# Index scores of a sparse-attention layer: two heads at once on 64 rows each, three products in place of two full-height ones

## What is computed

```python
dots = jnp.einsum('bqhd,bsd->bqhs', qi_b, k_idx) * idx_scale      # 8 index heads of 64
score = jnp.einsum('bqh,bqhs->bqs', wi_b, jax.nn.relu(dots))      # sum over the heads
score = jnp.where(causal, score, -jnp.inf)
_, sel = lax.top_k(score, topk)                                   # 256 keys per query
```

## Time and profile before

| | us |
|---|---|
| median of 3 runs | 732.51 (732.18 to 734.01) |
| the profiled execution | 737.07 |
| its span | 735.3 |
| TensorE matmul busy | 669.7 (91%) |
| TensorE weight loads busy | 552.7 (75%) |
| VectorE busy | 492.1 (67%) |
| ScalarE busy | 364.9 (50%) |
| GpSimd busy | 235.4 (32%) |

### The profile page before, as it was taken

One profiled execution on the slowest core, in us unless ns is written; L12 is line 12 of the kernel. 1 busy time (PEld: TensorE's weight loads), 2 busy tenths in 40 slices (PEclk: granted clock), 3 DMA queues, 4 the chain that ended last, 5 costly groups with the idle time before them and its releaser, 6 DMA issues.

```text
span 735.3 us, 8771 instructions
## 1 busy us (share of the span) xinstructions
PE 669.7 (91%) x3170; PEld 552.7 (75%) x3170; DVE 492.1 (67%) x737; ACT 364.9 (50%) x550; POOL 235.4 (32%) x113
## 2 busy tenths in 40 slices
PE   0489999899999999999999989998999988979996
PEld 0478988678888888888888877886777666758885
DVE  4786815677888899998079550014898988485734
ACT  1484435555563143452444434535787787783212
POOL 0003324432224152757766488420011110030000
PEclk9999999999999999999999999998999999989998
DMA  8902287353222110111100462075744340301531
GB/s 343 412 26 86 63 212 141 114 171 113 90 86 87 57 56 32 57 36 50 58 29 29 137 196 69 1 171 163 239 115 116 87 115 9 107 29 58 172 115 57
DMA packets 22661, 79.14 MB, mean 108 GB/s; under 512 B 3738, under 2 KB 4058, under 8 KB 21596
## 3 DMA queue, kind: packets, MB, share of 16 engines
q1 hardware_dynamic: 22620, 78.60, 35.2%
HBM read 61.77 MB, written 13.41 MB: 102 GB/s over the span
## 4 chain that ended last, share of the span: by engine, by line
PE 79%; DVE 8%; ACT 5%; issue 5%; DMA 2%; SPq 0%; ACTq 0%; DVEq 0%
PE ps L631 17%; PE ps L632 17%; PE ps L633 17%; PE ps L810 4%; PE ps L812 4%; PE ps L811 4%; PE ps L748 3%; DMA wa<-in_w_ada 2%; PE ps L689 2%; PE ps L690 2%; PE ps L670 2%; PE ps L671 2%; DVE phL L1384 2%; DVE acc L1178 1%; PE ps L761 1%
## 5 line engine op out<-in xcount | busy, mean ns | idle before, releaser
L631 PE MATMUL ps<-hH,wH 128*128 128x512 f32 (+1 forms) x592 | 230.3, 389 | 3.8 <-ACT wH L865 2.3
L632 PE MATMUL ps<-hL,wH 128*128 128x512 f32 (+1 forms) x592 | 228.3, 386 | 0.0
L633 PE MATMUL ps<-hH,wL 128*128 128x512 f32 (+1 forms) x592 | 228.1, 385 | 0.0
L1533 POOL TENSOR_TENSOR wL<-raw,wH 128x1024 fp32r<-128x1024 f32 x37 | 94.4, 2552 | 186.5 <-ACT wH L865 186.5
L631 PEld LDWEIGHTS ps<-hH,wH 128*128 128x128 f32 x592 | 111.9, 189 | 25.1 <-issue 3.0
L633 PEld LDWEIGHTS ps<-hH,wL 128*128 128x128 f32 x592 | 111.9, 189 | 21.5
L632 PEld LDWEIGHTS ps<-hL,wH 128*128 128x128 f32 x592 | 112.1, 189 | 19.2
L1376 DVE CUSTOM_DVE_ANT_0 ps<-ps,bias 128x128 f32<-128x128 f32 (+3 forms) x64 | 48.7, 761 | 45.6 <-PE ps L671 43.7
L1384 DVE TENSOR_TENSOR phL<-ps,phH 128x512 fp32r<-128x512 f32 (+1 forms) x96 | 52.7, 555 | 22.6 <-ACT phH L1040 18.5
L1020 ACT ACTIVATE relu<-ps,wabs 128x384 f32<-128x384 f32 (+5 forms) x48 | 40.1, 849 | 43.6 <-PE ps L690 17.5
L1270 DVE SCALAR_TENSOR_TENSOR score<-relu,wsgn,score 128x384 f32<-128x384 f32 (+5 forms) x42 | 49.7, 1183 | 17.2 <-ACT relu L1020 14.5
(11 more groups left out here) (206 smaller groups left out, 1102.9 us busy)
## 6 DMA issues: line engine op xcount, KB each, us to landing
raw<-in_w_units SPq DMA_DIRECT2D x36, 512.0 KB, 3.3
wa<-in_w_ada SPq DMA_DIRECT2D x8, 1024.0 KB, 8.8
ks<-qk_halves SPq DMA_DIRECT2D x32, 256.0 KB, 5.5
xin<-in_x SPq DMA_DIRECT2D x8, 512.0 KB, 12.5
gw<-in_w_ada SPq DMA_DIRECT2D x8, 512.0 KB, 4.4
qs<-qk_halves SPq DMA_DIRECT2D x16, 256.0 KB, 4.0
wo<-in_w_out SPq DMA_DIRECT2D x8, 512.0 KB, 9.3
xe<-in_x SPq DMA_DIRECT2D x8, 512.0 KB, 4.1
```

What stands on the lines that cost most here:

```text
L631: pe.matmul(out, wH[:, n % 2, kt, :], hH[:, kt, cols], start=(kt == 0), stop=False)
L632: pe.matmul(out, wH[:, n % 2, kt, :], hL[:, kt, cols], start=False, stop=False)
L633: mm = pe.matmul(out, wL[:, n % 2, kt, :], hH[:, kt, cols], start=False, stop=(kt == KT - 1))
L1533: g.tensor_tensor(wL[:, n % 2, :, :], raw[:, n % NRAW, :, :], wH[:, n % 2, :, :].bitcast(F32), ALU.subtract).then_inc(s_wL, 1)
```

## The change

The two heads of a pair are computed at once. `iqs` now has, for a pair of heads, the even head's rows in partitions 0 to 63 and the odd head's in 64 to 127, with the high and the low parts side by side in the free dimension and not over each other. `index_scores(i, pair)` makes three products per part of up to 512 keys: high by high, low by high and high by low; the fourth, low by low, is left out. Each is done for the even head on rows 0 to 63 into banks 4 and 5, then for the odd one on rows 64 to 127 into banks 6 and 7, in turn. The loop in `unit` issues a pair where it issued the even head, so pairs stand after steps 1, 5, 9 and 13 (block 2: 5, 8, 11 and 14). A pair waits for `s_relu` to reach u, so for both ReLUs of the pair before. The rotated rows come back by four DMAs.

```diff
-        iqs = at("iqs", [P, NIH, S - IQ0], F32R, 113)
+        iqs = at("iqs", [P, NIH // 2, 2, S - IQ0], F32R, 113)
...
-                                dst = iqs[HD * half + d:HD * half + d + k, h, :].bitcast(F32)
+                                dst = iqs[HD * (h % 2) + d:HD * (h % 2) + d + k, h // 2, half, :].bitcast(F32)
...
                     for half in range(2):
-                        sp.dma_start(iqs[HD * half:HD * half + ROPE, :, :].bitcast(F32),
-                                     diq[half].rearrange("h r s -> r h s")).then_inc(s_iqr, 16)
+                        for e in range(2):
+                            sp.dma_start(iqs[HD * e:HD * e + ROPE, :, half, :].bitcast(F32),
+                                         diq[half].rearrange("(p e) r s -> e r p s", e=2)[e]).then_inc(s_iqr, 16)
...
                         while b and at_step > first and scored * (2 * KT - first) < blocks * NIH * (at_step - first):
-                            index_scores(b + scored // NIH, scored % NIH)
-                            scored += 1
+                            index_scores(b + scored // NIH, scored % NIH // 2)
+                            scored += 2
...
-            def index_scores(i, h):
+            def index_scores(i, pair):
                 n = (i + 1) * P
-                u = NIH * (i - 2) + h
+                u = NIH * (i - 2) + 2 * pair
                 if u == 0:
                     pe.wait_ge(s_kidup, 16 * 8)
-                    pe.wait_ge(s_iqr, 32)
+                    pe.wait_ge(s_iqr, 64)
...
-                if u >= 2:
-                    pe.wait_ge(s_relu, u - 1)
-                dst = two(4 + 2 * (u % 2))
+                else:
+                    pe.wait_ge(s_relu, u)
                 for o in range(0, n, HALF):
                     e = min(n, o + HALF)
-                    q = iqs[:, h, P * i - IQ0:P * i - IQ0 + P]
-                    pe.matmul(dst[:, o:e], q, iks1[:, o:e], start=True, stop=False)
-                    mm = pe.matmul(dst[:, o:e], q, iks2[:, o:e], start=False, stop=True)
-                mm.then_inc(s_idx, 1)
+                    for m, (part, keys) in enumerate(((0, iks1), (1, iks1), (0, iks2))):
+                        for half in range(2):
+                            r = slice(HD * half, HD * half + HD)
+                            mm = pe.matmul(two(4 + 2 * half)[:, o:e], iqs[r, pair, part, P * i - IQ0:P * i - IQ0 + P], keys[r, o:e],
+                                           start=(m == 0), stop=(m == 2))
+                            if m == 2 and e == n:
+                                mm.then_inc(s_idx, 1)
```

## The result

The changed kernel takes 741.91 us (median of 6 runs, 738.56 to 742.85), the kernel before 732.88 (6 runs, 732.18 to 734.01). The medians lie 9.0 us apart. The ratio of the runs is 1.0106, 95% interval 1.0081 to 1.0131: slower by 7.8 us, between 5.9 and 9.6. The forecast was 741.5.

The account below looks back on a forecast made before the run. TensorE sets the pace while the scores run. Added waits, slots and form cost blocks 2 to 7 +1.3, +1.9, +1.35, +1.5, +1.45 and +1.55, together +9.0 us on 732.51: 741.5 us, range 736.5 to 753.5.

Parts of the forecast that it names:

- The wait for ReLU 3: Third pair (heads 4 and 5) waits for head 3's ReLU; units of blocks 3 to 7 last 17.74 to 19.71 us.
- a sign of being wrong: Units shorter than 16.6 us, no ReLU wait in blocks 5 to 7, or a loss outside 120 to 230 us.
- The slots: Score matmuls: three slots of two matmuls replace four matmuls per 512 columns and two heads; 0.224 to 0.227 us each.
- my middle value: Two weight loads per slot take 0.22 us, binding under 384, 256 or 128 columns; 1.36 us per pair in blocks 4 to 7.
- In and out of the form: Entering and leaving the 64-row form at each of 24 calls: 0.35 us added per pair, bounds 0 and 0.5.
- The clock: No further half-clock stretch after new waits; one or two more could add 0 to 3.4 us, up to 745, chance 0.10.
- No cost for the DMAs: Two more DMAs for turned rows delay SP's queue about a microsecond; first score call needing them is over 20 us later.
- the whole sum passed on: After block 7 VectorE's threshold search shifts along with TensorE, so the whole +9.0 us reaches the kernel's time.
- A: Rival: row halves of the score matmuls don't overlap, six matmuls for four; +20.3 us, 752.8 us, chance 0.17.
- B: Rival: quarter of score matmuls saved, no price for the 64-row form, waits remain; +2.6 us, 735.1 us, chance 0.06.
- C: Rival: faster, a quarter of 31.5 us of score matmuls (7.9 us) saved without the ReLU chain hindering; 724.6 us, chance 0.04.

## Why the prediction was right, and where it was not

The time was hit within 0.5 us and the mechanism is the one forecast. That the number came so close is in part luck: some of the terms were off in opposite directions, and the ratio of the runs is 7.8 us with an interval of 3.7.

*The wait for ReLU 3.* Right in kind and place, and in size in blocks 3 and 7. Forecast were 17.74, 17.72, 18.06, 18.89 and 19.71 us for the units of blocks 3 to 7; measured 17.8, 16.5, 17.2, 18.5 and 19.8. Block 4 has no wait at all, and its 16.5 lies below the 16.6 that the prediction had named as a sign of being wrong; the reason is the slots, below. The experiments on banks and on GpSimd's subtraction each remove the waits by what makes them, and each gives back its time.

*The slots.* Wrong: I took 0.22 us per slot as the floor, two loads one after the other at the spacing of 128-row loads. But the two loads of a slot, one for each half of the rows, start together: in block 7 the first two stand at 211.06 and the next two at 211.17, 0.11 us later. So slots of 256 and 384 columns cost their width, and a pair costs 1.41, 1.46 and 1.65 us in blocks 4 to 6 (from the first to the second pair of a unit, less four steps of 0.68) where I had 1.71. The forecast for these units was 1.2, 0.8 and 0.4 us too long. In block 4, where nothing waits, four pairs of 0.3 us too much are all of it; in blocks 5 and 6 two pairs make 0.5 and 0.1, and ReLU 3, which ended another 0.3 us earlier than I had taken (9.5 and 10.4 after the unit's start), makes the rest.

The Trainium skill's rule that a weight load depends on columns only (TensorE: Matmul & The Clock Gate, LDWEIGHTS) is not against these loads: on the same 64 rows they follow each other 0.11 us apart, as loads of 128 rows do. So my middle value did not follow from the rule; what was wrong was to let the two halves load in turn. The eight-row loads of the earlier trace rows, 0.064 us apart, stay outside of the rule.

*In and out of the form.* I took 0.35 us per pair from the eight-row transposes; calls show 0.42, the doubled entries 0.45. Forecast direction and size right, a little short. In blocks 5 to 7 a pair costs as much as two heads did before (1.46, 1.65 and 1.81 against 1.43, 1.64 and 1.81): the saved quarter and the price of the form cancel almost exactly. In block 3 it is 1.12 against 0.91.

*The clock.* I took no further stretch at half clock. The granted clock was 0.80 over the 17 us from 123 us on, against 0.88 over 14 before: 3.4 us in place of 1.7. It was block 2, with 3.38 us of wait, which I had charged with today's 1.7 us only. Not all of it was lost: the clock was down (0.88) already in the stretch from 129 to 132 us, in which TensorE waited. So block 2 took 1.8 us more where I had 1.3. In block 3 and block 7 nothing followed in this profile. Where the half clock falls is not fixed by the waits alone: with the same waits, the kernel with one head after the other shows 0.90 from 123 to 140 us and 0.91 from 140 to 160.

*No cost for the DMAs, and the whole sum passed on.* The first holds in the changed kernel's profile. But the 20 us that I gave as room are counted to the issue of the DMAs: in two profiles of kernels with the old layout the first score call waited 2.27 and 3.23 us for the queries, so the place has little room. The second held in both kernels with four banks: they gained 4.9 and 8.9 us, within the ranges worked out from their units alone, so nothing of it was lost behind them.

*Rivals.* A (no overlap) is refuted by the calls of 1.6 us, and the change does what it says. B's prices for the slots were right (1.04, 1.07, 1.23 and 1.36 us; the calls less 0.42 give 0.99, 1.04, 1.23 and 1.39), but not its missing price of the form. C needed ReLU 3 before 8.8 us after the unit's start; in the run with the short subtraction it ends at 9.4 in block 7, all waits are gone, and even there the form is not faster than the full-height products.

The sum by the trace up to block 7 is +7.3 us, the forecast was +9.0, and the runs say +9.0 by their medians and +7.8 by their ratio. The forecast was 2.4 us too long in blocks 4 to 6 and 0.5 too short in block 2. The missing 1.7 us lies within the interval of the runs and is not settled: runs of the changed kernel spread from 738.6 to 742.9, and the two fastest of the six have the highest granted clocks, 0.992 and 0.988 against 0.981 to 0.986.

## What to carry to other kernels

Before two pieces of work are joined into one, look at who frees their buffers: the pair asks for its later half's buffer at its earlier half's time, and if that chain has 0.2 us of slack the join costs microseconds, whatever it saves on the engine. Two half-height matmuls do run together, but each visit to the 64-row form costs about 0.43 us here, so it pays only for calls well above 1.7 us of full-height work, or where several calls can share one visit (not tried here). And where a tile needs only half of its banks, let the halves go round: here that was worth 4.9 us in the kernel before.

## What the runs showed of the hardware that I had not expected

- Matmuls on different 64 rows start together (0.01 us apart or less) in both orders of issue that were tried; three of one half before three of the other cost the same 1.59 us as in turn. Their weight loads start together too (two at 211.06, two at 211.17).
- A border between the 128-row and the 64-row form costs time on both sides, 0.42 to 0.45 us per visit in all, and the weights are not loaded ahead across it: 0.35 and 0.36 us of idle time on the loading side. That the one is the cause of the other is not shown.
- An accumulation on VectorE that runs beside GpSimd's subtraction in SBUF ends only after it: three took 6.00 us where the subtraction took 2.84, and 4.06 us where it took 0.76.
